# ConvFFN gate and up: twelve seven-product tiles in pairs in place of nine, with half of the activation forms made during the memory output projection

## What is computed

```python
x = x + _mem_attend(_rmsnorm(x, lp['g_mem_q']), mem_k, mem_v, lp['w_mq'], lp['w_mo'])
f, conv_state = _conv_ffn(_rmsnorm(x, lp['g_ffn']), conv_prev, lp['w_gate'], lp['w_up'],
                          lp['conv_w'], lp['conv_b'], lp['w_down'])
...
def _conv_ffn(h, prev, w_gate, w_up, conv_w, conv_b, w_down):
    gate_in = h @ w_gate
    buf = jnp.concatenate([prev, gate_in], axis=1)
    conv = conv_b
    for j in range(CONV_W):
        conv = conv + conv_w[j] * buf[:, j:j + t]
    out = (jax.nn.gelu(conv) * (h @ w_up)) @ w_down
    return out, buf[:, -(CONV_W - 1):]
```

## Time and profile before

| | us |
|---|---|
| median of 3 runs | 863.42 (862.41 to 865.62) |
| the profiled execution | 864.71 |
| its span, first to last instruction | 862.9 |
| PE busy in the span | 826.4 (96%) |
| DVE, ACT, POOL busy | 508.9 (59%), 371.3 (43%), 168.0 (19%) |

### The profile page before, as it was taken

One profiled execution on the slowest core, in us unless ns is written; L12 is line 12 of the kernel. 1 busy time (PEld: TensorE's weight loads), 2 busy tenths in 40 slices (PEclk: granted clock), 3 DMA queues, 4 the chain that ended last, 5 costly groups with the idle time before them and its releaser, 6 DMA issues.

```text
span 862.9 us, 17192 instructions
## 1 busy us (share of the span) xinstructions
PE 826.4 (96%) x7402; PEld 782.7 (91%) x7402; DVE 508.9 (59%) x787; ACT 371.3 (43%) x564; POOL 168.0 (19%) x133
## 2 busy tenths in 40 slices
PE   5999999998999999998999988999999999999996
PEld 4989999887989999984599988999999999999995
DVE  6969998898358535132234887777777758210013
ACT  6534415667646225122323744444444456322221
POOL 4100001110540342420044000000000024645430
PEclk9999999999999999999999998999999999999998
DMA  9211212635555493319213313232232341433302
GB/s 331 74 51 49 75 50 102 198 99 170 174 175 160 140 417 111 98 61 412 89 49 99 98 50 99 98 99 98 98 99 98 99 147 50 147 98 99 103 2 99
DMA packets 31293, 104.99 MB, mean 122 GB/s; under 512 B 3930, under 2 KB 7002, under 8 KB 28786
## 3 DMA queue, kind: packets, MB, share of 16 engines
q1 hardware_dynamic: 31218, 103.90, 35.5%
HBM read 96.28 MB, written 6.71 MB: 119 GB/s over the span
## 4 chain that ended last, share of the span: by engine, by line
PE 80%; DVE 9%; ACT 5%; DMA 4%; issue 1%; SPq 1%; POOL 0%; DVEq 0%; ACTq 0%
PE pj L694 17%; PE pj L696 16%; PE pj L695 16%; PE aux L701 4%; PE aux L702 4%; PE aux L703 4%; DMA w_raw<-in 3%; PE pj L1312 2%; PE aux L1243 2%; PE pj L701 1%; PE pj L703 1%; PE pj L702 1%; DVE h_lo L1886 1%; PE pj L1020 1%; DVE w_lo L1895 1%
## 5 line engine op out<-in xcount | busy, mean ns | idle before, releaser
L694 PE MATMUL pj<-h_hi,w_hi 128*128 128x260 f32 x816 | 233.8, 286 | 11.7 <-POOL w_lo L658 10.1
L696 PE MATMUL pj<-h_hi,w_lo 128*128 128x260 f32 x816 | 230.8, 283 | 0.0
L695 PE MATMUL pj<-h_lo,w_hi 128*128 128x260 f32 x768 | 217.0, 283 | 0.0
L658 POOL TENSOR_TENSOR w_lo<-w_raw,w_hi 128x512 fp32r<-128x512 f32 x90 | 124.7, 1408 | 374.8 <-ACT w_hi L1455 374.7
L694 PEld LDWEIGHTS pj<-h_hi,w_hi 128*128 128x128 f32 x816 | 154.0, 189 | 14.3 <-POOL w_lo L658 10.1
L1455 ACT ACTIVATE w_hi<-w_raw 128x1024 fp32r<-128x1024 f32 x82 | 86.7, 1057 | 182.3 <-PE pj L696 144.0
L696 PEld LDWEIGHTS pj<-h_hi,w_lo 128*128 128x128 f32 x816 | 154.0, 189 | 0.0
L695 PEld LDWEIGHTS pj<-h_lo,w_hi 128*128 128x128 f32 x768 | 144.9, 189 | 0.3
L658 POOL TENSOR_TENSOR wx_lo<-w_raw,wx_hi 128x512 fp32r<-128x512 f32 x28 | 36.8, 1336 | 262.7 <-ACT wx_hi L1455 262.7
L694 PE MATMUL pj<-h_hi,wx_hi 128*128 128x260 f32 x240 | 68.0, 283 | 0.0
L696 PE MATMUL pj<-h_hi,wx_lo 128*128 128x260 f32 x240 | 67.8, 283 | 0.0
(11 more groups left out here) (461 smaller groups left out, 2119.4 us busy)
## 6 DMA issues: line engine op xcount, KB each, us to landing
w_raw<-in SPq DMA_DIRECT2D x126, 512.0 KB, 3.6
caches<-in SPq DMA_DIRECT2D x14, 1024.0 KB, 11.9
vpg<-in SPq DMA_DIRECT2D x16, 256.0 KB, 3.0
kpg<-in SPq DMA_DIRECT2D x12, 256.0 KB, 3.0
x<-in SPq DMA_DIRECT2D x4, 520.0 KB, 7.7
out<-x SPq DMA_DIRECT2D x16, 130.0 KB, 1.9
out<-kT SPq DMA_DIRECT2D x1, 1040.0 KB
far<-in SPq DMA_DIRECT2D x1, 1024.0 KB, 5.0
```

The lines of the kernel that those rows point to most:

```text
L658: nc.gpsimd.tensor_tensor(lo[:, part], w_raw[:, raw_of(n) % 4, part], hi[:, part].bitcast(F32), ALU.subtract).then_inc(lo_done, 1)
L694: pe.matmul(out, s_hi, m_hi_, start=first, stop=False)
L695: pe.matmul(out, s_hi, m_lo_, start=False, stop=False)
L696: ins = pe.matmul(out, s_lo, m_hi_, start=False, stop=last)
```

## The change

Three edits go together.

1. `SEVEN` has twelve tiles, 3, 4, 6, 7, ..., 18, 19, so each turn of the loops on ACT and DVE is now a plain tile c and a pair a = c + 1, b = c + 2. The MLP has 68 units instead of 62.
2. The activation forms are laid out by feature tile k (four, each with four quarters) instead of by form, so they can be made in four steps. `scale_pair(k)`, `sum_form(k)`, `high_form(k)` and `low_form(k)` for k = 0 and 1 run in steps 4, 5 and 6 of the memory output projection; those for k = 2 and 3 come after it, the high parts ahead of `root`.
3. The low parts of the four units of tiles 1 and 2 go from DVE to POOL. Those of tile 0 and of tiles 3 to 20 stay on DVE.

```diff
-SEVEN = tuple(range(3, 20, 2))
+SEVEN = tuple(t for t in range(3, 20) if t % 3 < 2)
+F_COPIED, F_SUMMED, F_HIGH, F_DONE = (2, 5, 8, 10), (3, 7, 11, 14), (3, 6, 11, 12), 16
-DVE_LOWS = (... + (N_MQ, N_MQ + 1) + tuple(range(N_GU, UNIT[FT - 1])))
+DVE_LOWS = (... + (N_MQ, N_MQ + 1, N_GU, N_GU + 1) + tuple(range(UNIT[3], UNIT[FT - 1])))
 # PE, seven_products
-                    pe.wait_ge(h_split, 36)
+                    pe.wait_ge(summed, F_DONE)
 # ACT
+            def scale_pair(k):
+                for i in range(2):
+                    kt = k + i * (KT // 2)
+                    nc.scalar.activation(hg[:, k, 2 * i:2 * i + 2, :], halves(x[:, kt, :]), ACT.Copy,
+                                         scale=col("g_ffn", kt)).then_inc(ff_copied, 1)
+            def high_form(k):
+                act.wait_ge(summed, F_SUMMED[k])
+                nc.scalar.activation(f_hi[:, k], f_sum[:, k], ACT.Copy).then_inc(ff_copied, 1)
             def residual(base, j0, group, gain, passed):
                 for s in range(8):
...
                     square(x[:, s, :], T, j0 + s)
+                    if base == N_MO and s in (5, 6):
+                        high_form(s - 5)
+                    if base == N_MO and s in (4, 5):
+                        scale_pair(s - 4)
                 if base == N_MO:
                     high(N_GU + 2)
-                    for kt in range(KT):
-                        nc.scalar.activation(hg[:, kt, :], x[:, kt, :], ACT.Copy, scale=col(gain, kt)).then_inc(
-                            ff_copied, 1)
+                    scale_pair(2)
+                    scale_pair(3)
+                    high_form(2)
+                    high_form(3)
                     high(N_GU + 3)
                 root(group, halves(rinv[:, :]), sums01, D)
 # DVE
+            def sum_form(k):
+                dve.wait_ge(ff_copied, F_COPIED[k])
+                first = F_SUMMED[k] - 2
+                tt(f_sum[:, k, 0:4:3, :], hg[:, k, 0:4:3, :], hg[:, k, 1:2, :].broadcast_to([P, 2, HALF]),
+                   ALU.subtract).then_inc(summed, 1)
+                dve.wait_ge(summed, first)
+                stt(out=f_sum[:, k, 1, :], ...).then_inc(summed, 1)
+                dve.wait_ge(summed, first + 1)
+                stt(out=f_sum[:, k, 2, :], ...).then_inc(summed, 1)
+            def low_form(k):
+                dve.wait_ge(ff_copied, F_HIGH[k])
+                tt(f_lo[:, k], f_sum[:, k], f_hi[:, k].bitcast(F32), ALU.subtract).then_inc(summed, 1)
             def residual(base, group, j0, gain, at_):
...
                     add_square(j0 + s, s == 0, T, group)
+                    if base == N_MO and s in (5, 6):
+                        low_form(s - 5)
+                    if base == N_MO and s in (4, 5):
+                        sum_form(s - 4)
 # DVE, the loop: the pair's part
-            for t in range(2, FT - 2, 2):
+            for c in range(2, FT - 2, 3):
+                a, b = c + 1, c + 2
...
+                low_seven(a, 3)
+                read_first(a)
+                low_seven(b, 0)
+                read_mid(a)
+                low_seven(b, 1)
+                read_last(a)
+                low_seven(b, 2)
+                first_taps(a)
+                low_seven(b, 3)
+                read_first(b)
+                multiply(a)
```

More of the change, by code:

```diff
@@ L233, in build @@
         with ExitStack() as under:
-            hg = sbuf(under, "hg", [P, KT, T])
-        f_hi = sbuf(ffctx, "f_hi", [P, 4, KT // 2, HALF], F32R)
+            hg = sbuf(under, "hg", [P, KT // 2, 4, HALF])
+        f_hi = sbuf(ffctx, "f_hi", [P, KT // 2, 4, HALF], F32R)
         with ExitStack() as under:
-            f_sum = sbuf(under, "f_sum", [P, 4, KT // 2, HALF])
-        f_lo = sbuf(ffctx, "f_lo", [P, 4, KT // 2, HALF], F32R)
+            f_sum = sbuf(under, "f_sum", [P, KT // 2, 4, HALF])
+        f_lo = sbuf(ffctx, "f_lo", [P, KT // 2, 4, HALF], F32R)
         wx_hi = sbuf(ffctx, "wx_hi", [P, 2, 1024], F32R)
@@ L1368, in moving @@
                 def moving(k):
-                    return f_hi[:, i, k, :], f_lo[:, i, k, :]
+                    return f_hi[:, k, i, :], f_lo[:, k, i, :]
                 return moving
@@ L1460, in high_seven @@
                 if i in (1, 2):
[L1461 removed]
+                    act.wait_ge(summed, F_DONE + 3 * s + i + 1)
                     src = w_sum[:, 2 - i, :]
@@ L1805, in _ @@
             high(UNIT[2] + 1)
-            for i in range(4):
-                act.wait_ge(summed, 4)
-                nc.scalar.activation(f_hi[:, i], f_sum[:, i], ACT.Copy).then_inc(h_hi_done, 1)
             def copy_chain(t, i):
@@ L1820, in _ @@
             ff_open(1)
-            for t in range(2, FT - 2, 2):
[L1822 to L1836, removed]
+            for c in range(2, FT - 2, 3):
+                a, b = c + 1, c + 2
+                if c > 2:
+                    last_tap(c - 1)
+                high_seven(a, 1)
+                if c > 2:
+                    ff_open(c - 1)
+                high_seven(a, 2)
+                last_tap(c)
+                ff_open(c)
+                high_seven(a, 3)
+                copy_chain(a, 0)
+                high_seven(b, 0)
+                copy_chain(a, 1)
+                copy_chain(a, 2)
+                high_seven(b, 1)
+                high_seven(b, 2)
+                last_tap(a)
+                high_seven(b, 3)
+                copy_chain(b, 0)
+                ff_open(a)
+                high(UNIT[c + 3])
+                copy_chain(b, 1)
+                copy_chain(b, 2)
+                high(UNIT[c + 3] + 1)
+                if c + 4 in SEVEN:
+                    high_seven(c + 4, 0)
                 else:
-                    high(UNIT[t + 3])
+                    high(UNIT[c + 4])
             high(UNIT[FT - 1] + 1)
@@ L2453, in read_mid @@
                 dve.wait_ge(chain_done, 3 * s + 3)
-                dve.wait_ge(ff_copied, KT + 3 * s + 3)
+                dve.wait_ge(ff_copied, F_HIGH[3] + 3 * s + 3)
+                if s >= 1:
+                    dve.wait_ge(a_made, SEVEN[s - 1] + 1)
                 stt(out=up_last, in0=ff_bank(t, 0), scalar=-1.0, in1=lone_q,
@@ L2477, in _ @@
             order.done(tt(conv_past[:, 0], conv_past[:, 0], conv_past[:, 1], ALU.add))
[L2478 to L2489, removed]
+            sum_form(2)
+            sum_form(3)
+            low_form(2)
+            low_form(3)
             inverted(5)
-            low(UNIT[1] + 1)
             evict_gate(0)
             first_taps(0)
-            low(UNIT[2])
             multiply(0)
-            low(UNIT[2] + 1)
             evict_gate(1)
@@ L2500, in _ @@
             multiply(1)
[L2501 to L2524, removed]
+            for c in range(2, FT - 2, 3):
+                a, b = c + 1, c + 2
+                sum_corners(a)
+                if c > 2:
+                    first_taps(c - 1)
+                sum_rest(a)
+                low_seven(a, 0)
+                if c > 2:
+                    multiply(c - 1)
+                low_seven(a, 1)
+                evict_gate(c)
+                low_seven(a, 2)
+                first_taps(c)
+                sum_corners(b)
+                sum_rest(b)
+                multiply(c)
+                low_seven(a, 3)
[9 more added lines that the diff above has]
+                multiply(a)
+                low(UNIT[c + 3])
+                read_mid(b)
+                low(UNIT[c + 3] + 1)
+                read_last(b)
             first_taps(FT - 3)
```

22 lines of the change are left out of this document (13 added, 9 removed).

## The result

The kernel after the change takes **857.26 us** in the median (856.82 to 857.81), the kernel before it 862.91 beside it: a ratio of 0.9925 [0.9901, 0.9949]; the medians lie 5.6 us apart. (A ratio here is an estimate with its interval and not the quotient of the two medians, which is 0.9935.) A second set of runs on another chip gave 857.37 against 864.26, 0.9926 [0.9912, 0.9940], 6.9 us apart. The profiled execution of after took 857.32, its span is 855.5; before it was 864.71 and 862.9, so the two profiled executions lie 7.4 us apart.

The account below looks back on a forecast made before the run. PE, busy 96% of the span, was taken as the bound, with one MLP stall costing 7.6 us. Terms -7.6, +1.3, +3.1 and -4.3 gave -7.5 us: 863.4 to 855.9 us, range 852.5 to 859.5.

Parts of the forecast that it names:

- the forecast's own range: Whole kernel: 854.5 to 857.3 us around the forecast of 855.9, given a chance of 0.42.
- the rival with the fallen clock: Behind the wait for `root`: clock falls, next 3 to 5.6 us at half speed, 857.4 to 858.7 us; chance 0.24.
- The stall of tile 3 goes (-7.6): First copy in tile 3: PE's lost 4.94 us and 2.7 us at lower clock behind it disappear.
- 36 matmuls (-4.3): Three more tiles with 84 instead of 96 matmuls, at 0.12 us each: -4.3 us.
- The pairs run without a stall (0): Paired tiles a and b: b's copies have about 0.9 us of slack, so the pairs cost nothing.
- The small and the slower rival: Six pairs stall: small, 0.4 to 1 us each, 858.3 to 861.9, chance 0.08; slower, 868 at 2 us each, chance 0.04.
- `h_lo` late (+1.3): End of memory output projection: new forms start `h_lo` 1.75 us late against 0.45 slack, so PE stands 1.3 us.
- `root` late (+3.1): Ahead of tile 1: POOL's two halves hold DVE, `root` ends at 493.5, PE stands 3.1 us.
- A halved rate: POOL meeting DVE: alternative to whole-instruction turns; wait ahead of tile 1 would be 1.9 us, time 854.7 us.
- The lighter-holds rival: DVE's consecutive instructions keep POOL off; `root` only 0.6 to 1.5 us late, time 852.5 to 854.5; chance 0.18.
- The clock at `root` stays up: Behind the 3.1 us wait ahead of tile 1: forecast priced no clock loss.
- The sum: Profiled execution: -7.5 us in all, own time 857.2, span 855.4, tile starts 493.6, 516.6 and 526.7.

Follow-up runs that it names:

- POOL's units alone: Kernel before the change with only the low parts of tiles 1 and 2 moved to POOL: 866.07 us, 1.0019.
- the forms behind the projection: Changed kernel with `root` ahead of the `f_hi` and all forms made after the memory output projection: 858.66 us, 0.9938.
- the kernel with nine tiles: Changed kernel with before's nine tiles of seven products and their loops, forms and POOL's units kept: 861.59 us, 0.9972.
- the padded kernels: Changed kernel with one or three unused 520-column DVE additions ahead of `first_taps(a)` in each pair: 857.94 us and 865.04 us.
- three additions: Changed kernel with three unused 520-column DVE additions ahead of `first_taps(a)` in each pair: 865.04 us, 1.0012.
- `low_form(1)` alone moved: Changed kernel with `low_form(1)` on DVE moved from step 6 to behind the last square of step 7: 859.42 us, 0.9953.
- both moved: Changed kernel with `root` ahead of the high forms, and `high_form(1)` and `low_form(1)` both only in step 7: 852.21 us, 0.9866.
- both moves: Changed kernel with `root` ahead of the high forms and `low_form(1)` behind the last square of step 7: 854.33 us, 0.9884.
- one addition: Changed kernel with one unused 520-column DVE addition ahead of `first_taps(a)` in each pair: 857.94 us, 0.9923.

## Why the prediction held, step by step

It said 855.9 (852.5 to 859.5), faster. The median is 857.3: right in sign and inside the range, 1.4 us too low. It lies at the upper edge of the forecast's own range (854.5 to 857.3), and just below the 857.4 at which the rival with the fallen clock begins; it is after's profile, with the clock at 1.00 behind the wait, that speaks for the forecast and not the median.

- **The stall of tile 3 goes (-7.6): right.** No wait there, in after and in all versions with the new forms. But the prediction drew its cause as DVE's load in general, POOL's share included. The run with POOL's units alone shows that this edit by itself takes nothing from the stall (+0.9), so the new forms have a part in it. Whether they are enough alone, with the low parts still on DVE, wasn't run, except for unit 60: with it on DVE no wait in tile 3 came back. And the run with the forms behind the projection shows that a stall can also go from tile 3 by moving to tile 2.
- **36 matmuls (-4.3): right**, 4.2 measured by the kernel with nine tiles.
- **The pairs run without a stall (0): right**, and the 0.9 us of slack reckoned by laying out the orders is 0.85 in the trace for the copy, and about 1.1 by the padded kernels for the chain. The small and the slower rival are ruled out for this kernel; the latter's mechanism is real, and three additions a pair bring the time back to before's.
- **`h_lo` late (+1.3): right**, 1.2 measured. What it left out is that `high_form(1)` on ACT stands right behind as the next limit: with `low_form(1)` alone moved 0.7 us stayed, with both moved 0.17.
- **`root` late (+3.1): right in mechanism, 2.8 in size.** The two `conv_past` were held for whole instructions of POOL: they end 0.2 us behind POOL's first and second half, at 485.24 and 486.60, and last one half of POOL (1.3) and a little each. With unit 60 on DVE they took 0.33. A halved rate would have given the 0.33 us instructions 0.66. The rule cited for it, of the Trainium skill (SBUF — State Buffer, "SBUF: two separate sides"), agrees with these rows. The lighter-holds rival is out.
- **The clock at `root` stays up: half right.** It stayed in four profiled executions of five with this wait and fell in one, where it cost 1.55 us. So the rival with 0.24 doesn't stand against the forecast as another outcome; it happens to some executions of the same kernel.
- **The sum** came out as reckoned in the profiled execution: span 855.5 for 855.4, own time 857.3 for 857.2, starts of tiles 1, 3 and 4 within 0.1 us. **The step that failed is the last one**, from the profiled execution to the median: I took 1.3 us off because before's profiled run lay that much above its median. After's lay on it. That distance is scatter of one execution (before's runs reach from 862.3 to 867.4) and doesn't carry over. Without it the forecast would have been 857.2. So the gain in the medians, 5.6 us and 6.9 on another chip, is smaller than the 7.5 that were forecast and the 7.6 between the two profiles. Of the stall's 7.6 us 2.7 were the fallen clock, seen in one profile of before; in how many executions of before it falls there isn't on record.

## What to carry to other kernels

Where orders are written by hand, lay out each engine's list against the consumer's times and look at what stands between the input of a step and the instruction that releases PE: here moving one call (`root`) ahead of a wait was worth 2.8 us and two more moves 1.2 us on top, together nearly as much as three cheaper tiles (4.2). Work given to an idle POOL isn't free when DVE is in a chain: count what POOL's instructions hold, not only what DVE is spared. A delay pushed back helps only if nobody waits where it lands, and where the clock falls behind a wait, the wait can cost half as much again (1.55 us on 2.8), in some executions and not in others, so read its price off several executions.

## What was not expected of the hardware

- The clock's fall behind a wait isn't fixed by the wait's length. Behind 2.8 us lost it stayed at 1.00 four times and fell once; behind 3.7 (forms behind the projection), 3.9 (`low_form(1)` late), 4.9 (before) and 5.9 us (POOL's units alone) it fell in the profiled executions; after two waits of 1.5 and 2.9 us, 2.9 us of work apart, it stayed in one. The lower level lasted 3.5 us behind the waits up to 3.9 us and 6.9 us behind the two longest, where it began while PE still stood. The clock also fell behind shorter waits: all 14 profiled executions have two of them near 390 us, of 1.3 to 2.1 and 1.8 us from matmul to matmul, with 0.6 to 0.7 us between them, and behind them it fell for 3.5 us in five (before, after, both moves, one addition, POOL's units alone). Why the same wait has two outcomes isn't settled: from the start of the projection to the end of the wait PE takes 62.75 us in the one execution of after and 62.76 in the other.
- A 176-column operation of DVE took 1.45 us beside POOL and 0.33 alone; four `f_lo` of 1040 columns took 6.88 beside POOL and 4.68 alone. A unit of 2.5 us on POOL cost DVE 2.1 to 2.2, nearly all of it.
